# Experts in units of 512 gate or 512 up columns, own buffers for the last down weights, and a scatter in fp32r

## The chip, the cores and the metric

The kernel runs on one core of one Trainium2 chip, in one launch. The metric is the device time of that launch in microseconds. Engines: TensorE (PE, its weight loads PEld), VectorE (DVE), ScalarE (ACT), GpSimd (POOL) and SyncE (SP), which issues nearly all DMAs. A name with q (SPq) is the sequencer of an engine.

## The reference

Two transformer blocks on 256 tokens of 1,024 features, in fp32. The first block has two layers: attention and a dense SwiGLU of 3,584 columns, then attention and a mixture of eight SwiGLU experts. The second block adds a context stream, a SwiGLU of 2,816 columns for both streams (ff0c, ff0x), a long convolution, a differential attention, and a last SwiGLU (ff1). What matters here is the mixture:

```python
def moe_swiglu(h, router, wg, wu, wd):
    logits = (h @ router).astype(jnp.float32)
    top_vals, top_idx = lax.top_k(logits, TOP_K)          # 2 of 8
    gates = jax.nn.softmax(top_vals, axis=-1)
    gate_e = jnp.sum(jax.nn.one_hot(top_idx, N_EXPERTS, dtype=jnp.float32) * gates[..., None], axis=-2)
    out = jnp.zeros_like(h)
    for e in range(N_EXPERTS):
        out = out + gate_e[..., e:e + 1] * swiglu(h, wg[e], wu[e], wd[e])   # (silu(h @ wg) * (h @ wu)) @ wd
    return out
```

## The kernel before

**Products.** Weights come as fp32 and are multiplied as fp32r in three products: high x high, high x low, low x high. So each weight tile is split on the chip: ScalarE copies it to fp32r (the high part), VectorE subtracts that from the original (the low part).

**A block of a SwiGLU.** `feed` (on TensorE, ScalarE and VectorE, each with its own version) runs over blocks of 256 hidden columns (FB); an expert has NB1 = 14 of them, ff0c, ff0x and ff1 have NB2 = 11. The A tile of a block holds 256 gate and 256 up columns next to each other, 2 MB; it lands in `ringA` (two buffers) in two halves h of four row groups, each half as one DMA of gate and one of up with rows of 1 KB. The split halves lie in `As`, which has one buffer for each half. The B tile holds 256 rows of the down weights, 1 MB, lands in `ringB` (two buffers) and is split into `Bs` (one buffer).

**Order on TensorE.** In body n: `gu` of half 0 (12 matmuls of 512 columns), `turn` (two transposes of the hidden block n-1), `gu` of half 1 (12), `down` of block n-1 (12, added up in PSUM banks 4 to 7). For the experts there is one token tile (T = 1) of up to 128 gathered tokens; elsewhere there are two (T = 2), with twice as many matmuls for the same weights.

**Order on ScalarE in body n.** `hidden` (high part of the transposed block n-1), A half 0 of tile n+1 (L1497, waits A_lo_free, which TensorE raises after half 0), silu of block n (L1535), A half 1 of tile n+1 (waits tile_done), and B(n) into `Bs` (L1545, waits down_done of block n-1).

**Order on VectorE in body n.** `hidden` (low part, L2092, raises hdT_ready), A half 0 (L2077, raises A_split), silu times up (L2108), A half 1, B(n) (L2114, raises B_low), and then what `after(n)` adds: in bodies 2 and 3 the addition of the previous expert's rows to x (L2150), in body 3 the one-hot columns (`one_hot`, L2130 to L2137), in body 12 the gathered tokens (`dispatch`).

**Order on SyncE.** `load_experts` (L569 to L607) issues A(2i), B(2i-1), A(2i+1), B(2i) in a loop. A(n) waits for A_split of tile n-2, half by half; B(n) waits for B_low of block n-2. After the last expert `load_ffn` issues the loads of ff0c.

**Experts.** One expert follows the other without a break. For each, `gather` picks its tokens with one-hot matmuls. After its last down, `keep_y` (ScalarE, L1574, in body 1 of the next expert) copies the result out of PSUM and frees the banks (acc_free). `scatter` (TensorE, L884, after bodies 2 and 3 of the next expert) multiplies it in fp32 with `selgT`: the one-hot matrix that carries the gates, transposed by TensorE at block 12 (L897) and copied by ScalarE in body 13 (L1585).

**The end of a stage.** Where `drains` holds (dense, last expert, ff0x, ff1), the last block's `turn` and `down` stand alone behind body nb-1, with four idle products (L690) between them. Its Bs copy waits until the down before it is done. A second path for more than 128 tokens per expert (`all_tokens`) is in the program and is not taken with these inputs: the trace shows the gather of the first one.

## Time and profile before

| What | us |
|---|---|
| Median of 3 runs | 2700.34 |
| The runs | 2695.68, 3695.21, 2700.34 |
| The profiled execution | 2695.8 |
| Its span, first to last instruction | 2694.0 |
| TensorE busy in the span | 2573.2 (96%) |
| VectorE busy | 1820.4 (68%) |
| ScalarE busy | 1456.5 (54%) |

The span holds 34,481 instructions and the mean granted clock of TensorE is 0.975 of full speed. The mixture of experts runs from about 605 to 1643 us. The DMAs move 631.66 MB, of which the experts' weights are the greater part: 224 loads of gate and 224 of up with 512 KB each, 112 of down with 1 MB.

How to read it: a busy share is an average over stages with different limits. In a row of the timeline the first number is the start, the second the duration (of a group of like instructions, if xN is more than 1), and the brackets tell how long the engine was idle before it and what ended that. Matmuls overlap in the records, so the pace is read from start to start.

### The profile page before, as it was taken

The page shows a single profiled execution, that of the slowest core. Times are in us where ns is not written, and L with a number is a line of the kernel's source. Part 1 is how long each engine was busy: PE and PEld are TensorE (multiplying, and loading weights), DVE is VectorE, ACT ScalarE, POOL GpSimd, SP SyncE. Part 2 cuts the span into 40 slices and gives each one's busy share as a digit, 9 for nine tenths or more (in the row PEclk, how much of TensorE's full clock was granted, in tenths as well). Part 3 has the DMA queues.
Part 4 walks back from the last instruction along what each step waited for, and adds up shares of the span by engine and source line. Part 5 has one row for each costly group of instructions (what it writes and reads, how often), then busy time and mean ns, then how long its engine had stood idle before and what let it go on. Part 6 is the DMA issues. An engine that isn't in the chain of part 4 may idle for free.

```text
span 2694.0 us, 34481 instructions
## 1 busy us (share of the span) xinstructions
PE 2573.2 (96%) x11981; PEld 2031.8 (75%) x11981; DVE 1820.4 (68%) x1810; ACT 1456.5 (54%) x1677; POOL 52.2 (2%) x40
## 2 busy tenths in 40 slices
PE   7899999878999999999999998999999999998998
PEld 6678887656878787878888886888884687776786
DVE  6454446548888988888888885545444475776544
ACT  4544434535677777777777675445333243466443
POOL 0000000015000000000000000000000000000000
PEclk9999999879999999999999999999999999998999
DMA  6865542659999999999999996555543344435551
GB/s 217 290 219 187 187 156 87 241 179 308 367 336 353 348 351 349 352 349 351 349 346 355 339 343 203 181 185 184 183 156 108 102 142 127 130 107 179 184 186 60
DMA packets 446014, 631.66 MB, mean 234 GB/s; under 512 B 17672, under 2 KB 345896, under 8 KB 445736
## 3 DMA queue, kind: packets, MB, share of 16 engines
q1 hardware_dynamic: 445064, 627.36, 69.5%
q0 software_dynamic: 864, 3.15, 0.3%
q8 instruction: 55, 0.90, 0.1%
q14 instruction: 31, 0.25, 0.0%
HBM read 629.40 MB, written 1.05 MB: 234 GB/s over the span
## 4 chain that ended last, share of the span: by engine, by line
PE 87%; DVE 6%; ACT 4%; issue 2%; DMA 1%; SPq 0%; DVEq 0%; ACTq 0%
PE ps L806 39%; PE ps L834 20%; PE ps L1188 6%; PE ps L740 5%; PE ps L1215 2%; PE ps L1120 2%; PE ps L819 2%; PE ps L930 1%; PE ps L871 1%; DVE As L2077 1%; PE ps L1179 1%; DVE ringL L2047 1%; PE ps L884 1%; ACT Bs L1545 1%; ACT As L1497 1%
## 5 line engine op out<-in xcount | busy, mean ns | idle before, releaser
L2077 DVE TENSOR_TENSOR As<-ringA,As 128x2048 fp32r<-128x2048 f32 x318 | 735.2, 2312 | 212.4 <-ACT As L1497 203.5
L806 PE MATMUL ps<-As,xgs 128*128 128x512 f32 x2688 | 666.1, 397 | 6.7 <-DVE As L2077 4.1
L1497 ACT ACTIVATE As<-ringA 128x2048 fp32r<-128x2048 f32 x318 | 608.0, 1912 | 22.7 <-DMA ringA<-in_dense_w_up 9.9
L834 PE MATMUL ps<-Bs,hds 128*128 128x512 f32 x2472 | 590.0, 391 | 12.3 <-DVE hds L2092 12.3
L806 PEld LDWEIGHTS ps<-As,xgs 128*128 128x128 f32 x2688 | 494.7, 188 | 117.5 <-issue 14.3
L834 PEld LDWEIGHTS ps<-Bs,hds 128*128 128x128 f32 x2472 | 464.1, 188 | 116.5 <-issue 9.2
L2114 DVE TENSOR_TENSOR Bs<-ringB,Bs 128x2048 fp32r<-128x2048 f32 x159 | 368.8, 2320 | 157.4 <-ACT Bs L1545 156.8
L1545 ACT ACTIVATE Bs<-ringB 128x2048 fp32r<-128x2048 f32 x159 | 304.9, 1918 | 215.6 <-PE ps L834 215.4
L806 PE MATMUL ps<-As,xs 128*128 128x512 f32 x1632 | 392.3, 397 | 10.8 <-DVE xs L2015 6.8
L806 PEld LDWEIGHTS ps<-As,xs 128*128 128x128 f32 x1632 | 306.3, 190 | 78.3 <-issue 7.6
L1518 ACT ACTIVATE hds<-ps 128x256 fp32r<-128x256 f32 x206 | 73.9, 383 | 317.5 <-PE ps L819 282.8
L1535 ACT ACTIVATE sg<-ps 128x256 f32<-128x256 f32 x206 | 79.1, 384 | 192.9 <-PE ps L806 168.7
L2092 DVE TENSOR_TENSOR hds<-ps,hds 128x256 fp32r<-128x256 f32 x206 | 82.2, 418 | 90.1 <-ACT hds L1518 89.5
L2047 DVE TENSOR_TENSOR ringL<-ringA,ringH 128x2048 fp32r<-128x2048 f32 x42 | 96.1, 2290 | 57.3 <-ACT ringH L1477 57.1
L740 PE MATMUL ps<-As,xs 128*128 128x512 f32 (+1 forms) x384 | 118.7, 393 | 9.4 <-DVE ringL L2047 5.6
L2108 DVE TENSOR_TENSOR hh<-sg,ps 128x256 f32<-128x256 f32 x206 | 85.3, 415 | 55.8 <-ACT sg L1535 55.7
L1477 ACT ACTIVATE ringH<-ringA 128x2048 fp32r<-128x2048 f32 x42 | 80.2, 1911 | 79.2 <-PE ps L1188 57.7
L806 PE MATMUL ps<-As,hcTR 128*128 128x512 f32 x352 | 111.6, 398 | 0.0
L740 PEld LDWEIGHTS ps<-As,xs 128*128 128x128 f32 x384 | 73.8, 198 | 25.1 <-DVE ringL L2047 6.0
L1188 PE MATMUL ps<-ringL,hcTR 128*128 128x512 f32 x224 | 87.6, 391 | 0.0
L740 PE MATMUL ps<-ringL,xs 128*128 128x512 f32 (+1 forms) x224 | 87.2, 389 | 0.0
L1188 PE MATMUL ps<-ringH,hcTR 128*128 128x512 f32 x208 | 83.3, 401 | 0.8 <-DVE ringL L2047 0.8
(349 smaller groups left out, 2632.4 us busy)
## 6 DMA issues: line engine op xcount, KB each, us to landing
ringA<-in_moe_w_gate SPq DMA_DIRECT2D x224, 512.0 KB, 4.5
ringA<-in_moe_w_up SPq DMA_DIRECT2D x224, 512.0 KB, 5.6
ringB<-in_moe_w_down SPq DMA_DIRECT2D x112, 1024.0 KB, 6.2
ringA<-in_w_ff_in SPq DMA_DIRECT2D x132, 512.0 KB, 4.7
ringA<-in_w_in SPq DMA_DIRECT2D x56, 1024.0 KB, 5.3
ringA<-in_w_ada SPq DMA_DIRECT2D x36, 1024.0 KB, 6.2
ringB<-in_w_ff_out SPq DMA_DIRECT2D x33, 1024.0 KB, 5.0
ringA<-in_dense_w_gate SPq DMA_DIRECT2D x28, 512.0 KB, 3.6
```

Of the source, the lines that this page charges most:

```text
L740: m = mm(ps[:, 4 + 2 * (n % 2) + tt, 0:cols], xs[:, l, k, tt * P:(tt + 1) * P], w, start=k == 0 and m_ == 0, stop=k == KC - 1 and m_ == 2)
L806: m = mm(ps[:, bank, :], lhs(l, tt, k), As[:, h, r, k % 4, :], start=k == 0 and n == 0, stop=k == KC - 1 and n == 2)
L834: m = mm(ps[:, 4 + 2 * tt + half, :], hds[:, buf, l, q, :], Bs[:, q, r, half * 512:(half + 1) * 512], start=first and q == 0 and n == 0, s ...
L1188: m = mm(dst, lhs[l][:, k, tt * P:(tt + 1) * P], w[q], start=k == 0 and m_ == 0, stop=k == KC - 1 and m_ == 2)
L1477: A(high(p["name"], n, h)[:, :, 0:cols], ringA[:, a0 % 2, 4 * h:4 * h + 4, 0:cols], ACT.Copy).then_inc(A_high, 1)
L1497: A(As[:, h, 0, :, :], ringA[:, (p["a"] + u) % 2, 4 * h:4 * h + 4, :], ACT.Copy).then_inc(A_high, 1)
L1545: A(Bs[:, :, 0, :], ringB[:, b0 % 2, :, :], ACT.Copy).then_inc(B_high, 1)
L2047: V.tensor_tensor(ringL[:, a0 % 2, 4 * h:4 * h + 4, 0:cols], ringA[:, a0 % 2, 4 * h:4 * h + 4, 0:cols], f32(high(p["name"], n, h)[:, :, 0: ...
L2077: V.tensor_tensor(As[:, h, 1, :, :], ringA[:, (p["a"] + u) % 2, 4 * h:4 * h + 4, :], f32(As[:, h, 0, :, :]), ALU.subtract).then_inc(A_spli ...
L2092: V.tensor_tensor(flat(hds[:, buf, 1, :, :]), ps[:, 2 + tt, 0:FB], f32(flat(hds[:, buf, 0, :, :])), ALU.subtract).then_inc(hdT_ready, 2 // T)
L2108: V.tensor_tensor(hh[:, buf, :], sg[:, buf, :], ps[:, buf, FB:BW], ALU.mult).then_inc(h_ready, 2 // T)
L2114: V.tensor_tensor(Bs[:, :, 1, :], ringB[:, (p["b"] + u) % 2, :, :], f32(Bs[:, :, 0, :]), ALU.subtract).then_inc(B_low, 1)
```

## The change

1. Experts only: `load_experts` loads 512 gate columns as one tile (u = 0) and 512 up columns as the next (u = 1), each half with one DMA and rows of 2 KB. TensorE runs a new body: half 0, transposes of part u of the pair before, half 1, down of part u of the pair before. Silu and the product with up run once per pair over 512 columns. The down weights of block 2i+u are split in the body of unit 2i+1+u and used one unit later than before.
2. Where a stage drains, the last down weights are split into a place of their own (`down_home`): the high part into hTR or xs, the low part in place of the load in `ringB` (which ringH overlays). The idle products between are gone, and the downs of the block before are spread around the last transposes. For the experts' last pair this is done for its first part. The first B load of ff0c then waits until that part is done.
3. `selT` is now a matrix of 0 and 1 (VectorE compares the transposed selg with 0), the gate of each row is a sum in `small` (VectorE, `gate_sums`), `keep_y` scales by it and rounds to fp32r, `y_low` (VectorE) makes the rest and frees the banks, and `scatter` runs two fp32r matmuls for each half in place of one in fp32. `keep_y` moved from body 1 to body 2.

The path for more tokens (all_tokens) is changed in the same way. The core of the diff:

```diff
+        def down_home(p, b):
+
+            return by_rows(xs[:, 0, :, :] if p["name"] == "ff0x" else hTR[:, :, :]), by_rows(ringH[:, b % 2, :, :])
...
-        ye = ar(1024, D)
+        ye = arenaR[:, 1024:1024 + D], hTR[:, 0:4, :].rearrange("p k n -> p (k n)")
...
-        selgT = ar(2560, TILES, P)
+        selT = arenaR[:, 2560:2560 + TILES * P].rearrange("p (t s) -> p t s", t=TILES)
...
-                    n, a0 = i * 2 + u, p["a"] + u
-                    g, up = wg(e), wu(e)
+                    a0 = p["a"] + u
                     for h in range(2):
                         if isinstance(e, int) and isinstance(i, int) and i == 0:
                             half_free(a0, h)
                         else:
                             sp.wait_ge(A_split, e * (2 * nb) + i * 4 + (2 * (p["q"] + u) - 3 + h))
                         sl = slice(4 * h, 4 * h + 4)
-                        sp.dma_start(ringA[:, a0 % 2, sl, 0:FB], w2d(g)[:, sl, bass.ds(n * FB, FB)]).then_inc(A_full[a0 % 2][h], 16)
-                        sp.dma_start(ringA[:, a0 % 2, sl, FB:BW], w2d(up)[:, sl, bass.ds(n * FB, FB)]).then_inc(A_full[a0 % 2][h], 16)
+                        sp.dma_start(ringA[:, a0 % 2, sl, :], w2d((wg, wu)[u](e))[:, sl, bass.ds(i * BW, BW)]).then_inc(A_full[a0 % 2][h], 16)
...
-            load_ffn(ph["ff0c"], *g0)
+            load_ffn(ph["ff0c"], *g0, ring=(down_done, ph["ff0c"]["s"] - 2))
...
-                    if not lead:
+                    if last and drains:
+                        down(*prev, tts=(0,))
+                        turn(i, u)
+                        down(*prev, tts=(1,))
+                        down(i, u, weights=down_home(p, p["b"] + u))
+                    elif not lead:
                         down(*prev)
                     if after and isinstance(i, int):
                         after(2 * i + u)
-                    if last and drains:
-                        turn(i, u)
-                        idle_products(4)
-                        down(i, u)
...
-                    pe.wait_ge(selgT_ready, e + 1)
...
-                    last = mm(ps[:, 6 + half, :], selgT[:, tt, :], ye[:, half * 512:(half + 1) * 512], start=True, stop=True)
+                    for q in range(2):
+                        last = mm(ps[:, 6 + half, :], selT[:, tt, :], ye[q][:, half * 512:(half + 1) * 512], start=q == 0, stop=q == 1)
...
+                def body(i, u, last):
+                    lead = first and isinstance(i, int) and i == 0
+                    gate_or_up(e, i, u, 0, 1, lambda l, tt, k: xgs[:, l, k, :], 2 * e + 1, xg_split)
+                    if not lead:
+                        turn_part(e, i - 1, u, 1)
+                    gate_or_up(e, i, u, 1, 1, lambda l, tt, k: xgs[:, l, k, :], 2 * e + 1, xg_split)
+                    if last and final:
+                        down_part(e, i - 1, u, 1, qs=(0,))
+                        turn_part(e, i, 0, 1)
+                        pe.wait_ge(selgT_ready, e + 1)
+                        turn_part(e, i, 1, 1, 3, False)
+                        down_part(e, i - 1, u, 1, qs=(1,))
+                        down_part(e, i, 0, 1, down_home(moe, moe["b"]))
+                        down_part(e, i, 1, 1)
+                    elif not lead:
+                        down_part(e, i - 1, u, 1)
+                    if isinstance(i, int):
+                        after(2 * i + u)
+                blocks(pe, NB1, body, 2)
...
-                A(ye[:, :], ps[:, 4:6, :].rearrange("p a b -> p (a b)"), ACT.Copy).then_inc(acc_free, 1)
+                act.wait_ge(selgT_ready, e + 1)
+                A(ye[0], ps[:, 4:6, :].rearrange("p a b -> p (a b)"), ACT.Copy, scale=small[:, 354:355]).then_inc(y_high, 1)
...
+                def body(i, u, last):
+                    if isinstance(i, int):
+                        before(2 * i + u)
+                    lead = first and isinstance(i, int) and i == 0
+                    nxt = (i + 1, 0) if u else (i, 1)
+                    if not lead:
+                        part_high(e, i - 1, u, 1)
+                    unit_high(e, *nxt, 0)
+                    if last and not final:
+                        rows_part(e + 1, 0)
+                    if u == 0:
+                        gate_silu(e, i, 1)
+                    unit_high(e, *nxt, 1)
+                    if last and not final:
+                        rows_part(e + 1, 1)
+                    if last and final:
+                        down_high(e, i, 0, down_home(ph["moe"], ph["moe"]["b"])[0], 0)
+                        part_high(e, i, 0, 1)
+                        part_high(e, i, 1, 1, 3)
+                        down_high(e, i, 1, None, 2)
+                    elif u:
+                        down_high(e, i, 0)
+                    elif not lead:
+                        down_high(e, i - 1, 1)
+                blocks(act, NB1, body, 2)
...
+                def body(i, u, last):
+                    lead = first and isinstance(i, int) and i == 0
+                    nxt = (i + 1, 0) if u else (i, 1)
+                    if isinstance(i, int) and i == 1 and u == 0 and not first:
+                        y_low(e - 1)
+                    if last:
+                        gate_sums(e)
+                    if not lead:
+                        part_low(e, i - 1, u, 1)
+                    unit_low(e, *nxt, 0)
+                    if last and not final:
+                        rows_part(e + 1, 0)
+                    if u:
+                        gate_times_up(e, i, 1)
+                    unit_low(e, *nxt, 1)
+                    if last and not final:
+                        rows_part(e + 1, 1)
+                    if last and final:
+                        down_low(e, i, 0, down_home(ph["moe"], ph["moe"]["b"]))
+                        part_low(e, i, 0, 1)
+                        part_low(e, i, 1, 1, 3)
+                        down_low(e, i, 1)
+                    elif u:
+                        down_low(e, i, 0)
+                    elif not lead:
+                        down_low(e, i - 1, 1)
+                    if isinstance(i, int):
+                        after(2 * i + u)
+                blocks(dve, NB1, body, 2)
...
+            def gate_sums(e):
+
+                dve.wait_ge(selg_tp, e + 1)
+                V.tensor_reduce(small[:, 354:355], ps[:, 3, 0:TILES * P], X, ALU.add)
+                V.tensor_scalar(selT[:, :, :].rearrange("p a b -> p (a b)"), ps[:, 3, 0:TILES * P], 0.0, None, ALU.is_gt).then_inc(selgT_ready, 1)
+
+            def y_low(e):
+
+                dve.wait_ge(y_high, e + 1)
+                V.scalar_tensor_tensor(ye[1], ps[:, 4:6, :].rearrange("p a b -> p (a b)"), small[:, 354:355], f32(ye[0]), ALU.mult, ALU.subtract).then_inc(acc_free, 1)
```

## Rows read from the trace of the kernel before

**Rows 1.** Windows view, one expert: us, busy of each engine, TensorE clock, DMA share, GB/s.
```profile
859.80:986.00 126.20, 125.95 (x577) 102.21 (x576) 111.66 (x85) 90.57 (x75) 0.00 (x0) 1.00 1.02 350
```

**Rows 2.** Timeline of one block: start, us, engine, line, operation, count, idle before.
```profile
918.10 2.88 PE L806 MATMUL ps<-As,xgs 128*128 128x512 f32 x12
...
921.58 1.92 ACT L1497 ACTIVATE As<-ringA 128x2048 fp32r<-128x2048 f32 x1
...
923.52 2.29 DVE L2077 TENSOR_TENSOR As<-ringA,As 128x2048 fp32r<-128x2048 f32 x1 [0.65 <-ACT As L1497]
...
923.81 2.88 PE L834 MATMUL ps<-Bs,hds 128*128 128x512 f32 x12
...
926.05 0.37 SPq L582 DMA_DIRECT2D ringA<-in_moe_w_gate  x1
...
926.53 2.88 PE L806 MATMUL ps<-As,xgs 128*128 128x512 f32 x12
926.88 1.92 ACT L1545 ACTIVATE Bs<-ringB 128x2048 fp32r<-128x2048 f32 x1 [0.63 <-PE ps L834]
...
928.84 2.29 DVE L2114 TENSOR_TENSOR Bs<-ringB,Bs 128x2048 fp32r<-128x2048 f32 x1 [0.26 <-ACT Bs L1545]
...
931.38 0.37 SPq L590 DMA_DIRECT2D ringB<-in_moe_w_down  x1
```

**Rows 3.** Windows view: two microseconds of 1 KB rows, then two of 4 KB rows.
```profile
919.50:921.50 2.00, 2.00 (x11) 1.63 (x10) 1.56 (x2) 0.93 (x2) 0.00 (x0) 1.00 1.08 381
925.00:927.00 2.00, 2.00 (x11) 1.65 (x10) 1.87 (x3) 1.37 (x2) 0.00 (x0) 1.00 1.02 404
```

**Rows 4.** Timeline, end of the mixture stage: a B load, then A halves landing.
```profile
1611.85 0.38 SPq L590 DMA_DIRECT2D ringB<-in_moe_w_down  x1
...
1619.76 1.92 ACT L1497 ACTIVATE As<-ringA 128x2048 fp32r<-128x2048 f32 x1 [0.17 <-DMA ringA<-in_w_ff_in]
...
1624.11 1.91 ACT L1497 ACTIVATE As<-ringA 128x2048 fp32r<-128x2048 f32 x1 [1.46 <-DMA ringA<-in_w_ff_in]
```

**Rows 5.** Tile view of in_moe_w_down: time from issue to landing.
```profile
DMA to landing us min/median/max: 4.8/6.2/9.7
```

**Rows 6.** Timeline, units after the scatters of one expert.
```profile
1024.66 3.31 PE L806 MATMUL ps<-As,xgs 128*128 128x512 f32 x12
...
1034.83 3.31 PE L806 MATMUL ps<-As,xgs 128*128 128x512 f32 x12
...
1037.93 1.21 DVE L2150 TENSOR_TENSOR x<-x,ps 128x1024 f32<-128x1024 f32 x1
...
1040.79 0.41 DVE L2092 TENSOR_TENSOR hds<-ps,hds 128x256 fp32r<-128x256 f32 x1
...
1041.38 3.01 PE L834 MATMUL ps<-Bs,hds 128*128 128x512 f32 x12 [0.25 <-DVE hds L2092]
```

**Rows 7.** Chain of waits, end of dense and end of ff1: start, us, what.
```profile
400.65 5.47 PE ps L834 x24
...
408.68 1.28 ACT L1610
...
414.21 1.13 DVE x L2387
...
2670.76 5.47 PE ps L834 x24
...
2676.32 1.92 ACT Bs L1545
...
2680.94 3.07 PE ps L834 x12
...
2685.71 1.29 DVE xn L2735
```

**Rows 8.** Timeline, last block of the mixture stage.
```profile
1617.98 2.29 DVE L2114 TENSOR_TENSOR Bs<-ringB,Bs 128x2048 fp32r<-128x2048 f32 x1 [0.18 <-ACT Bs L1545]
...
1630.93 3.00 PE L834 MATMUL ps<-Bs,hds 128*128 128x512 f32 x12 [2.67 <-DVE hds L2092]
```

More of the change, by code:

```diff
@@ L381, in build @@
         ada("adar", 2, 16)
[L382 removed]
+        ffn("moe", NB1, NE, loads=1)
         ffn("ff0c", NB2)
@@ new lines, in turn_part @@
+            def turn_part(e, i, u, T, bank=2, follows=True):
+                for tt in range(T):
+                    pe.wait_ge(h_ready, ffn_count(moe, T, e, i, 1, tt))
+                    v = ffn_count(moe, T, e, i, u, tt, 1)
+                    if follows and started(v):
+                        pe.wait_ge(hdT_ready, v)
+                    for q in range(2):
+                        src = hh[:, u, q * P:(q + 1) * P] if T == 1 else hhW[:, tt, u * FB + q * P:u * FB + (q + 1) * P]
+                        m = tr(ps[:, bank if T == 1 else tt, q * P:(q + 1) * P], src, ident)
+                    m.then_inc(tp_done, 2 // T)
@@ new lines, in down_part @@
+            def down_part(e, i, u, T, weights=None, qs=range(2)):
+                first = isinstance(i, int) and i == 0 and u == 0
+                for tt in range(T):
+                    if first and tt == 0:
+                        pe.wait_ge(acc_free, e + moe["f"])
+                    pe.wait_ge(hdT_ready, ffn_count(moe, T, e, i, u, tt))
+                    if tt == 0:
+                        pe.wait_ge(B_low, e * NB1 + i * 2 + (moe["b"] + u + 1))
+                    for q in qs:
+                        for n, (l, r) in enumerate(((0, 0), (0, 1), (1, 0))):
+                            for half in range(2):
+                                m = mm(ps[:, 4 + 2 * tt + half, :], hds[:, u if T == 1 else tt, l, q, :], (Bs[:, q, r, :] if weights is None else weights[r][:, q, :])[:, half * 512:(half + 1) * 512],
+                                       start=first and q == 0 and n == 0, stop=q == 1 and n == 2, skip_group_check=True)
+                    if 1 in qs:
+                        m.then_inc(down_done, 2 // T)
@@ L862, in gather, with all_tokens @@
+            def all_tokens(e):
+                def body(i, u, last):
+                    for h in range(2):
+                        gate_or_up(e, i, u, h, 2, split_stream, 1, xr_split)
+                    if u:
+                        for part in range(2):
+                            turn_part(e, i, part, 2)
+                            down_part(e, i, part, 2)
+                blocks(pe, NB1, body)
             def gather(e):
@@ L1529, in body @@
                         split_rows(0)
+                    b0 = p["b"] + u
+                    if last and drains:
+                        act.wait_ge(B_full[b0 % 2], e * (8 * nb) + i * 16 + 16 * (b0 // 2 + 1))
+                        A(down_home(p, b0)[0], ringB[:, b0 % 2, :, :], ACT.Copy).then_inc(B_high, 1)
                     for tt in range(T):
@@ L1539, in body @@
                         split_rows(1)
-                    b0 = p["b"] + u
+                    if last and drains:
+                        hidden(i, u)
+                        return
                     act.wait_ge(B_full[b0 % 2], e * (8 * nb) + i * 16 + 16 * (b0 // 2 + 1))
@@ L1545, in body @@
                     A(Bs[:, :, 0, :], ringB[:, b0 % 2, :, :], ACT.Copy).then_inc(B_high, 1)
-                    if last and drains:
-                        hidden(i, u)
                 blocks(act, nb, body, head)
@@ new lines, in part_high @@
+            def part_high(e, i, u, T, bank=2):
+                p = ph["moe"]
+                for tt in range(T):
+                    act.wait_ge(tp_done, ffn_count(p, T, e, i, u, tt))
+                    v = ffn_count(p, T, e, i, u, tt, 3 - T)
+                    if started(v):
+                        act.wait_ge(down_done, v)
+                    A(hds[:, u if T == 1 else tt, 0, :, :].rearrange("p a b -> p (a b)"), ps[:, bank if T == 1 else tt, 0:FB], ACT.Copy).then_inc(hd_high, 2 // T)
@@ L2101, in body @@
                         split_rows(0)
+                    if last and drains:
+                        dve.wait_ge(B_high, e * nb + i * 2 + (p["b"] + u + 1))
+                        hi, lo = down_home(p, p["b"] + u)
+                        V.tensor_tensor(lo, ringB[:, (p["b"] + u) % 2, :, :], f32(hi), ALU.subtract).then_inc(B_low, 1)
                     for tt in range(T):
@@ L2440, in all_tokens, with body @@
                 def all_tokens(e):
-                    feed(p, 2, e, True)
+                    def body(i, u, last):
+                        nxt = (i + 1, 0) if u else (i, 1)
+                        if u:
+                            gate_times_up(e, i, 2)
+                        for h in range(2):
+                            unit_low(e, *nxt, h)
+                        if u == 0:
+                            down_low(e, i, 0)
+                        else:
+                            part_low(e, i, 0, 2)
+                            down_low(e, i, 1)
+                            part_low(e, i, 1, 2)
+                    blocks(dve, NB1, body)
+                    dve.wait_ge(down_done, e * (2 * NB1) + (p["s"] + 2 * NB1))
                     dve.wait_ge(acc_free, e + 1)
```

132 lines of the change are left out of this document (110 added, 22 removed).

## The prediction

> **What bounds the kernel now.** I read the windows view first, one window per expert. An expert of the middle of the mixture stage takes 126.2 us; TensorE is busy for 125.95 of them at full clock, VectorE for 111.66, and the DMA engines move 350 GB/s at a share of 1.02 [rows 1]. So TensorE sets this stage, eight experts long, and two others are close behind it. Which cover hides them, the timeline of one block tells [rows 2]. Count from the start of a block of 256 gate and 256 up columns (918.10). TensorE does 24 matmuls of gate and up, two transposes, 12 matmuls of down, and starts the next block at 926.53: 8.43 us a block. ScalarE splits the first half of the next tile from 921.58 (3.48 after the start), VectorE from 923.52 to 925.81, 0.7 us before the next block. VectorE's low part of the down weights runs at 928.84 to 931.13. SyncE reuses each buffer at once: the load of A's first half goes out at 926.05, that of B at 931.38. The rest of this text is about those slacks of half a microsecond.
>
> **The inner loop: nothing to gain on TensorE.** A unit is now 512 gate columns or 512 up columns, and two units make a pair. A pair has 48 matmuls of gate and up and 24 of down, as two blocks had; by [rows 2] it takes 2 x 8.43 us again. One silu and one product of 512 columns replace two of 256 each: some 0.2 us less per pair on ScalarE and on VectorE, both of which have idle time (126.2 - 111.66 = 14.5 us for VectorE in an expert [rows 1]). I cost it at nothing.
>
> **The loads: 1 KB rows become 2 KB rows, and SyncE's order turns against them.** The loads of A are half as many and longer; a stretch of 1 KB rows moves 381 GB/s, one of 4 KB rows 404 [rows 3]. The bytes stay. But the down matmuls of a unit now come one unit later: down_low for B(n) ran in VectorE's body n and now runs in body n+1. SyncE's program keeps its order: A(n+3) stands behind the load of B(n+1), which waits for that down_low. Before, the two A halves went out in the middle of the body (926.05 and 2.7 us later), ahead of B at 931.38. Now all three leave together, at 13.28 us from the start of unit n (931.38 - 918.10), with B first. Queued behind the waiting B are exactly A(n+3)'s two halves, and ScalarE waits for those. ScalarE wants A's first half in unit n+2, at 16.86 + 3.48 = 20.34, and VectorE's result then has about 0.45 us to spare: 2.29 us of work that begins 1.94 us after ScalarE's, with two handovers, against 8.43: of the 0.7 us that it ended early about 0.25 go into handovers. The budget from B's issue to A's landing is 20.34 + 0.45 - 13.28 = 7.5 us.
> What will it take? The trace has one such bunch, at the end of the stage: B goes at 1611.85, the first A half directly behind it, and ScalarE, which waited for it, starts at 1619.76, 7.9 us later; the second half follows at 1624.11 [rows 4]. That half was of 1 KB rows; at the rate of long rows 1.05 MB takes 2.60 us in place of 2.75, so 7.75. This is 0.25 to 0.3 over the budget, in a circle of two units (the bunch waits for TensorE's unit n, and TensorE's unit n+3 for the bunch; the down in between ties it to n+1), so 0.14 us a unit. Seven experts of 14 units give 98 x 0.14 = 14 us. Bounds: the quickest 1 MB load of B landed in 4.8 us [rows 5]; with 2.6 for the half behind it 7.4, so 0. The median is 6.2: 8.8 us, 1.3 over, 0.65 a unit, 64 us. I take 14, since the row of 1619.76 is the only one of this very order.
> The Trainium skill's page DMA: Bandwidth & Descriptors (Anatomy of one DMA) fits a transfer as 2.0 us plus its bytes at 436 GB/s. By that an estimate for both is 6.8 us, and the term would be 0; the bunch in [rows 4] took 7.9, so the trace is slower than the page here.
>
> **The scatter.** Each expert ends with two scatters of two fp32 matmuls. A block that follows one starts 10.17 us after the one before (1034.83 - 1024.66), so a scatter costs 10.17 - 8.43 = 1.74 us. Now it is four fp32r matmuls of 512 columns at 2.73/12 = 0.23 us: 0.92. That saves 0.82 twice per expert. VectorE pays for it. Added are y_low, a 128x1024 operation from PSUM like the 1.29 us of L2735 [rows 7], in unit 2 before part_low, and gate_sums (two passes over 256 columns, like the 0.41 of hds each [rows 6]) in unit 13. Removed is one ScalarE copy.
> Unit 2: B's low part starts 2.31 after the unit's start (928.84 - 926.53) and lasts 2.2 net of the overlap with the next row; y_low ends at 5.8, part_low at 6.2, TensorE sees it at 6.4. The down is due at 5.71 (923.81 - 918.10 [rows 2]): 0.67 us of wait. ScalarE's copy y_high (1.0 us, half of the 1.92 of the copy of 2048 columns at 926.88, behind its B copy that ends at 2.3) is hidden.
> Unit 4: before, the addition to x started 3.10 into the unit (1037.93), one-hot columns followed, and hds came at 1040.79; the down began at 1041.38 with 0.25 us of wait [rows 6]. The shorter scatter gives less time ahead of it: B's low part starts at 2.31 - 0.92 = 1.39, the addition at 3.6, hds at 3.6 + 2.86 = 6.46, ready at 7.05, due 5.71: 1.34 us. Scatter and waits cost 1.84 + 0.67 + 1.34 + 0.2 (gate_sums) = 4.05, before 3.48 + 0.25 = 3.73. Seven experts: +2 us. Bounds: no wait felt, 7 x -1.9 = -13; the same chain against a unit with A late, +6.
>
> **The ends of stages.** Dense, ff0x and ff1 end with a free-standing block: ScalarE's Bs copy waits for the last down (2676.32), VectorE follows, TensorE fills with idle products and starts the last down at 2680.94 [rows 7]. With an own buffer both parts are made earlier, under 11 us of gate and up. From 2670.76: down of one token tile 2.73, transposes 0.44, the other 2.73, so 2676.66: 4.3 us earlier in ff1 and in ff0x, which has the same chain. In dense another chain ends later: the next weights are split by ScalarE and VectorE before x is updated at 414.21. From 400.65 + 5.9 = 406.55 (the buffer of the second tile is free) 0.4 + 1.28 + 1.92 + 2.29 with handovers is 412.5, so 1.7 (0.4 for a part of 256 columns, 1.28 the table load at 408.68). Sum -10.3; bound -12.9, if dense gets all.
>
> **The end of the mixture stage** is where two edits meet. The last B load waited for down_low of block 11, done 1611.82. That now comes a unit later, at 1617.98 + 2.29 = 1620.27 [rows 8], less 2.73 because TensorE has done one down less by then: 1617.5. Behind it stand ff0c's first A loads, and ScalarE splits those before it touches down_home. With the bunch of [rows 4], the halves land 7.9 and 12.3 later, at 1625.7 and 1630.1. Then ScalarE: split to 1632.0, home copy to 1633.9, two parts, B copy to 1636.6; VectorE behind it: 1634.3, 1636.6, 37.0, 37.4, 1639.7; TensorE: down (6,0) at 37.1, down (6,1) at 1639.9. Before, the last down began at 1630.93 [rows 8]: 9.0 us later. y_low (1.3) lies under the three idle products; the last two scatters give 1.6 back. Term +7.4. Bounds: if the loads are in time, the same chain from 1621.7 ends 2.2 earlier, so -3.8; +9.
> The first expert has its own losses on VectorE while GpSimd works; the same operations stay, I cost it at 0, within 4 either way.
>
> **Sum.** -10.3 + 7.4 + 2 + 14 = +13. The profiled execution took 2695.8 us (span 2694.0), so 2709; it lay 4.5 below the median of 2700.34.
>
> **Rivals.**
> 1. The loads are in time. The inner loop holds 8.43; ends, scatter and drain as above: 2695.8 - 10.3 + 7.4 + 2 = 2695. For it: 2 KB rows, 7.4 us from the quickest loads. 0.27. The fit of the Trainium skill's page DMA: Bandwidth & Descriptors (Anatomy of one DMA) would give this case.
> 2. As 1, and VectorE's new work is hidden and the last drain is not held by loads: 2695.8 - 10.3 - 3.8 - 13 = 2669. Against it: 0.25 us of wait stood in unit 4 already. 0.10.
> 3. The other side: the bunch takes the median landing. Place: SyncE, A behind B in each unit. Price 64 us in place of 14: 2759. It decides from a landing of 8.6 us on, where 98 x 0.55 = 54 us is 2%. 0.15.
> 4. The change doesn't do what it says (fewer load instructions, no idle products): next to nothing, 0.03.
> The forecast itself: 0.45, with 2690 to 2735.
>
> **Numbers.** Range 2670 to 2759, from rival 2 to rival 3, leaves out about 0.2. Two per cent, about what a measurement of this kernel can tell, is 54 us. Faster by more: 0.02, since no case reaches 2646. Slower by more: most of rival 3, 0.13. Within: 0.85.
>
> **What would show it.** In the timeline of the middle of an expert, SyncE's issues stand in a bunch, B first, 13.3 us after the unit start (right or wrong at once); ScalarE's A copies name a DMA as what they waited for; TensorE's L806-like halves wait for As. Unit starts 8.43 apart there: rival 1. PE's waits for hds stand in units 2 and 4, 0.7 and 1.3 us. The last block of ff1 has no idle products and ends 4.3 us earlier against its gate and up. After the last expert's matmuls, ScalarE waits for in_w_ff_in before it copies down weights. Wrong it would be if the silu, longer by some 0.2 us, pushes A's second half over its slack of about half a microsecond, or if 2 KB rows start flowing sooner after their issue than 1 KB rows do.

## The result, and the profile after

The changed kernel takes 2710.41 us (median of 6 runs, 2708.38 to 2713.71), the kernel before 2698.34 in the same series (median of 5: a sixth run, of 3695 us, was disturbed and is left out): a ratio of 1.0047, 95% interval 1.0032 to 1.0063. So the change makes the kernel slower, by about half a per cent. The forecast was 2709.0, slower too, and within 2% of the kernel before. The profiled execution has a span of 2708.8 us, before 2694.0; the 14.8 us between these two are what the rows can explain.

To see where they lie, I cut both spans at the same instructions of TensorE: the start of the first gather, the two transposes of selg at the end of each expert (L897 before, L973 after), and the first matmul of ff0c, of ff0x (the first that reads hTR, 0.5 us after its very first) and of the convolution. One down (12 matmuls, 2.73 us) has moved from ahead of the expert's mark to behind it; the table puts it back.

| Stretch, us | before | after | difference | forecast |
|---|---|---|---|---|
| up to the first gather | 605.2 | 604.1 | -1.0 | -1.7 |
| first expert | 128.1 | 128.7 | +0.5 | 0 |
| the seven others | 882.5 | 901.0 | +18.5 | +16 |
| last mark to ff0c's first matmul | 32.7 | 37.4 | +4.8 | +7.4 |
| ff0c | 184.8 | 184.3 | -0.5 | 0 |
| ff0x with its end | 430.3 | 427.3 | -3.0 | -4.3 |
| the rest with ff1's end | 430.4 | 425.9 | -4.5 | -4.3 |

The windows view, one expert, answers to [rows 1]. The columns are the same.

```profile
988.43:1117.12 128.69, 126.18 (x575) 101.71 (x574) 111.44 (x80) 90.44 (x67) 0.00 (x0) 1.00 0.94 341
```

TensorE does the same number of matmuls at full clock and now stands still for 2.5 us in each expert (128.69 - 126.18), before for 0.25; the DMA share fell from 1.02 to 0.94. The timeline of the middle of an expert shows what it stands still for; it answers to [rows 2].

```profile
1189.64 0.37 SPq L602 DMA_DIRECT2D ringB<-in_moe_w_down  x1
...
1190.74 1.00 SPq L595 DMA_DIRECT2D ringA<-in_moe_w_gate  x2
...
1198.29 0.37 SPq L602 DMA_DIRECT2D ringB<-in_moe_w_down  x1
1198.31 1.92 ACT L1673 ACTIVATE As<-ringA 128x2048 fp32r<-128x2048 f32 x1 [1.17 <-DMA ringA<-in_moe_w_gate]
...
1200.26 2.29 DVE L2254 TENSOR_TENSOR As<-ringA,As 128x2048 fp32r<-128x2048 f32 x1 [1.90 <-ACT As L1673]
...
1202.61 3.06 PE L892 MATMUL ps<-As,xgs 128*128 128x512 f32 x12 [0.53 <-DVE As L2254]
...
1207.79 0.37 SPq L602 DMA_DIRECT2D ringB<-in_moe_w_down  x1
...
1208.90 1.00 SPq L595 DMA_DIRECT2D ringA<-in_moe_w_gate  x2
...
1211.22 2.88 PE L892 MATMUL ps<-As,xgs 128*128 128x512 f32 x12
```

Read it from left to right in time. B goes out at 1189.64 and A's two halves stand right behind it: the bunch. ScalarE has been waiting for 1.17 us when the gate half is there at 1198.31, 8.67 us after B's issue. VectorE's low part follows, and TensorE's unit starts 0.53 us late at 1202.61. The next unit starts 8.61 us after that, with no wait. Not every unit is late: of 97 distances between unit starts in the seven experts, 23 are over 0.25 us longer than the same ones of e1 (the same kernel without the bunch, below), 29 more by 0.1 to 0.25, and units 3 to 6 of an expert lose 0.2 us at the most.

The waits view of ScalarE and then of TensorE, from 735 to 1600 us (time in total, times, the longest). Before, TensorE's view of this stretch had one line, 1.5 us for hds. TensorE's 6.3 us for As are about a third of what the bunch costs; the rest doesn't show as a named wait (see e1).

```profile
ACT As L1673 <- DMA ringA<-in_moe_w_gate: 40.0, 51, 1.9
...
ACT As L1673 <- DMA ringA<-in_moe_w_up: 13.0, 25, 1.4
```

```profile
PE ps L922 <- DVE hds L2315: 10.1, 13, 1.1
PE ps L892 <- DVE As L2254: 6.3, 13, 1.2
```

The page's DMA issues (number, KB each, median from issue to landing) fit: an A half now takes 8.3 or 9.0 us, B 5.0.

```profile
ringA<-in_moe_w_gate SPq DMA_DIRECT2D x112, 1024.0 KB, 8.3
ringA<-in_moe_w_up SPq DMA_DIRECT2D x112, 1024.0 KB, 9.0
ringB<-in_moe_w_down SPq DMA_DIRECT2D x112, 1024.0 KB, 5.0
```

Units 2 and 4 after an expert's end, from the timeline; they answer to [rows 6].

```profile
1151.86 1.28 DVE L2430 SCALAR_TENSOR_TENSOR hTR<-ps,small,arenaR 128x1024 fp32r<-128x1024 f32 x1
...
1153.06 0.41 DVE L2315 TENSOR_TENSOR hds<-ps,hds 128x256 fp32r<-128x256 f32 x1
...
1153.60 3.01 PE L922 MATMUL ps<-Bs,hds 128*128 128x512 f32 x12 [0.59 <-DVE hds L2315]
...
1173.09 0.42 DVE L2315 TENSOR_TENSOR hds<-ps,hds 128x256 fp32r<-128x256 f32 x1
...
1173.69 3.00 PE L922 MATMUL ps<-Bs,hds 128*128 128x512 f32 x12 [1.06 <-DVE hds L2315]
```

y_low stands ahead of hds in unit 2 and TensorE waits 0.59 us; in unit 4 it waits 1.06. The forecast said 0.67 and 1.34.

The end of the mixture stage, from the chain of waits; it answers to [rows 4, 8].

```profile
1636.52 6.95 DMA ringA<-in_w_ff_in
...
1643.49 1.92 ACT As L1673
...
1647.64 0.69 DVE hh L2327
...
1648.38 1.11 PE ps L907 x4
...
1652.41 1.91 ACT Bs L1703
...
1654.35 2.30 DVE Bs L2334
...
1656.79 3.00 PE ps L922 x12
```

ScalarE waits until 1643.49 for ff0c's first half, as foreseen. VectorE's product with up (hh) stands in its program behind the low part of that same half, so the last transposes wait too, for 9.85 us, until 1648.38. The last down begins at 1656.79.

The end of ff1, from the chain of waits; it answers to [rows 7].

```profile
2690.02 2.74 PE ps L847 x12
2692.76 0.44 PE ps L831 x4
2693.20 5.52 PE ps L847 x24
...
2698.74 1.12 ACT xn L2151 x2
```

From the last gate and up to the norm it is 8.72 us; before, 13.27 (2670.76 to 2684.03).

### The profile page after: what moved, and what is told of

It reads as the page before. It is cut to its first block, busy times and chain, and to the rows that moved or that the text cites. A ratio compares the mean times of both kernels' runs of the same rounds, so it can differ in the third digit from the quotient of the medians.

```text
span 2708.8 us, 33553 instructions
## 1 busy us (share of the span) xinstructions
PE 2564.5 (95%) x11949; PEld 2026.9 (75%) x11949; DVE 1817.4 (67%) x1778; ACT 1455.6 (54%) x1613; POOL 51.2 (2%) x40
## 4 chain that ended last, share of the span: by engine, by line
PE 69%; DVE 12%; DMA 7%; ACT 6%; issue 5%; SPq 1%; DVEq 0%; ACTq 0%
PE ps L818 19%; PE ps L892 9%; PE ps L847 9%; DMA ringA<-in_moe_w_gate 6%; PE ps L1283 6%; PE ps L752 5%; PE ps L922 5%; DVE As L2254 4%; ACT As L1673 3%; DVE Bs L2334 2%; PE ps L1310 2%; PE ps L1215 2%; PE ps L1025 1%; PE ps L947 1%; PE ps L831 1%
## 5 line engine op out<-in xcount | busy, mean ns | idle before, releaser
L818 PEld LDWEIGHTS ps<-As,xs 128*128 128x128 f32 x1632 | 306.5, 190 | 75.5 <-issue 5.5
L922 PE MATMUL ps<-Bs,hds 128*128 128x512 f32 x1332 | 323.6, 392 | 11.8 <-DVE hds L2315 10.9
L922 PEld LDWEIGHTS ps<-Bs,hds 128*128 128x128 f32 x1332 | 249.5, 188 | 69.8 <-issue 17.6
L2334 DVE TENSOR_TENSOR Bs<-ringB,Bs 128x2048 fp32r<-128x2048 f32 x111 | 253.8, 2287 | 10.5 <-ACT Bs L1703 9.5
L847 PE MATMUL ps<-Bs,hds 128*128 128x512 f32 x1056 | 247.8, 390 | 0.0
L1703 ACT ACTIVATE Bs<-ringB 128x2048 fp32r<-128x2048 f32 x111 | 212.5, 1914 | 39.6 <-PE ps L922 39.1
L847 PEld LDWEIGHTS ps<-Bs,hds 128*128 128x128 f32 x1056 | 198.1, 188 | 41.8
L2298 DVE TENSOR_TENSOR Bs<-ringB,Bs 128x2048 fp32r<-128x2048 f32 x44 | 100.9, 2293 | 119.7 <-ACT Bs L1646 119.7
L1646 ACT ACTIVATE Bs<-ringB 128x2048 fp32r<-128x2048 f32 x44 | 84.3, 1916 | 135.4 <-PE ps L847 135.4
L1634 ACT ACTIVATE sg<-ps 128x256 f32<-128x256 f32 x94 | 36.1, 384 | 126.6 <-PE ps L818 125.6
```

The costliest lines, as they stand in the source:

```text
L818: m = mm(ps[:, bank, :], lhs(l, tt, k), As[:, h, r, k % 4, :], start=k == 0 and n == 0, stop=k == KC - 1 and n == 2)
L847: m = mm(ps[:, 4 + 2 * tt + half, :], hds[:, buf, l, q, :], w[:, half * 512:(half + 1) * 512], start=first and q == 0 and n == 0, stop=q = ...
L922: m = mm(ps[:, 4 + 2 * tt + half, :], hds[:, u if T == 1 else tt, l, q, :], (Bs[:, q, r, :] if weights is None else weights[r][:, q, :])[: ...
L1703: A(Bs[:, :, 0, :] if dst is None else dst, ringB[:, b0 % 2, :, :], ACT.Copy).then_inc(B_high, 1)
L2298: V.tensor_tensor(Bs[:, :, 1, :], ringB[:, (p["b"] + u) % 2, :, :], f32(Bs[:, :, 0, :]), ALU.subtract).then_inc(B_low, 1)
L2334: V.tensor_tensor(lo, ringB[:, (p["b"] + u) % 2, :, :], f32(hi), ALU.subtract).then_inc(B_low, 1)
```

## The experiments

Each kernel's ratio is to the kernel before on the same chip (median 2697.4 us in the first series, 2697.3 in the second). The stretches below are those of the table above, read in the same way from each kernel's profiled execution. e1 to e4 ran on one chip, e5 to e7 on another, and the changed kernel in a series of its own. A difference between two kernels can therefore be taken from the medians or from their ratios to the kernel before, and where the two disagree both are given.

| Kernel | median us | first gather | first expert | seven experts | end of mixture | ff0x | rest |
|---|---|---|---|---|---|---|---|
| before | 2698.3 | 605.2 | 128.1 | 882.5 | 32.7 | 430.3 | 430.4 |
| after | 2710.4 | 604.1 | 128.7 | 901.0 | 37.4 | 427.3 | 425.9 |
| e1 | 2691.5 | 599.5 | 126.1 | 883.1 | 37.7 | 430.4 | 426.0 |
| e2 | 2681.4 | 599.6 | 126.6 | 883.1 | 29.7 | 427.3 | 425.9 |
| e3 | 2736.1 | 604.9 | 132.0 | 917.1 | 34.9 | 430.4 | 430.5 |
| e4 | 2724.4 | 600.0 | 129.9 | 913.9 | 39.6 | 427.5 | 426.0 |
| e5 | 2686.3 | 604.0 | 126.2 | 885.0 | 29.2 | 429.7 | 426.0 |
| e6 | 2694.3 | 605.0 | 126.3 | 883.1 | 29.7 | 434.2 | 430.5 |
| e7 | 2679.3 | 603.6 | 125.5 | 882.3 | 28.5 | 426.9 | 426.3 |

### e1: A ahead of B on SyncE

The changed kernel with one difference: A(n+3) is issued ahead of B(n+1), whose wait ends later.

```diff
-                    with sp.Fori(1, nb // 2) as i:
-                        A(e, i, 0)
...
+                    with sp.Fori(1, m - 1) as i:
+                        A(e, i, 1)
                         B(e, i - 1, 1)
-                        A(e, i, 1)
+                        A(e, i + 1, 0)
                         B(e, i, 0)
```

> The changed kernel with one edit in SyncE's program of the mixture stage: the load of A(n+3) is issued ahead of that of B(n+1), so that A no longer stands behind a wait for down_low. Theory (the bunch of loads is what slows the inner loop): ScalarE's splits of A in the experts wait for no DMA any more, unit starts are 8.43 us apart again, an expert takes 126.4 us from gather to gather in place of 128.9 (before: 126.14, less 1.6 for the scatters, plus some 2 of waits for hds in units 2 and 4), six of them give 15 us, the first and the last expert some 2 to 3 more: about 2692 us against 2710. The end of the stage keeps its loss, since ff0c's loads still stand behind the last B. Rival (VectorE's added work, y_low and gate_sums, is what costs, and the loads only look late): the experts stay at 128 us or more, 2705 to 2710.

Measured: 2691.46 us, ratio 0.998 (0.997 to 0.999). In SyncE's timeline A's halves no longer leave right behind B; they go when their own buffers come free.

```profile
1190.53 0.37 SPq L602 DMA_DIRECT2D ringB<-in_moe_w_down  x1
1193.85 3.32 SPq L595 DMA_DIRECT2D ringA<-in_moe_w_up  x2
```

ScalarE's waits view names no DMA from 735 to 1600 us, and an expert takes 126.28 us by the windows view:

```profile
849.08:975.36 126.28, 124.78 (x576) 102.06 (x575) 111.73 (x80) 89.91 (x67) 0.00 (x0) 1.00 0.96 349
```

This settles the cause of the loss: seven experts take 883.1 us in place of 901.0, the kernel 18.9 less (18.1 by the ratios). Nothing but the order of issues on SyncE is different. Of the 17.8 us, TensorE stood still for 9.0 (901.0 - 882.2 against 883.1 - 873.4 in the windows view of the seven experts); the other 8.8 lie in its busy time, with as many matmuls at the same granted clock of 1.00. Part of that shows in the records: the 12 matmuls of a first half that starts after a pause take 2.88 us up to the next group in the mean, in e1 a first half takes 2.74. ScalarE waited for second halves too (29 of its 76 waits ended 10 us or more after B's issue), but TensorE's pauses for As are all ahead of a first half. What is left above before in the seven experts is 0.7 us, the scatter with its waits.

### e2: A ahead of B at the end of the stage too

e1, with ff0c's first two A tiles issued ahead of the experts' last two B loads.

```diff
                     B(e, m - 2, 1)
                     if not last:
                         A(e + 1, 0, 0)
+                    elif tail:
+                        tail(0)
                     B(e, m - 1, 0)
...
                 run(NE - 1, NE - 2, True)
+                if tail:
+                    tail(1)
                 B(NE - 1, m - 1, 1)
...
-            load_experts(ph["moe"], one(t["moe_w_gate"]), one(t["moe_w_up"]), one(t["moe_w_down"]))
+            load_experts(ph["moe"], one(t["moe_w_gate"]), one(t["moe_w_up"]), one(t["moe_w_down"]), lambda k: load_ffn(ph["ff0c"], *g0, part=k))
```

> As the run with A first, and also at the end of the stage: ff0c's first two A tiles are issued ahead of the last two B loads of the last expert. Theory: ScalarE doesn't wait for in_w_ff_in in the last block, the last down starts some 9 to 10 us earlier, and part of that reaches the end of the launch: about 2683 us. Rival (the end is set by the row of ScalarE and VectorE work in the drain, not by the loads): no more than 2 us better than the run with A first.

Measured: 2681.41 us, ratio 0.9946 (0.9927 to 0.9965). By the timeline the transposes of the last pair wait 1.12 us for hh instead of 9.85. TensorE then waits 2.69 us for hds, which VectorE makes behind its low parts of ff0c's A tile and of the down weights:

```profile
1615.20 0.65 PE L927 MATMUL ps<-c,hh 128*128 128x128 f32 x4 [1.12 <-DVE hh L2347]
...
1619.94 1.22 PE L942 MATMUL ps<-hTR,hds 128*128 128x512 f32 x2 [2.69 <-DVE hds L2335]
...
1624.39 2.93 PE L942 MATMUL ps<-Bs,hds 128*128 128x512 f32 x12
```

The end of the mixture stage takes 29.7 us in place of 37.7: the 8.0 us were the wait for in_w_ff_in. The medians are 10.0 us apart, the ratios 9.2, the profiled executions 10.4; of the latter 8.0 lie here and 3.1 in ff0x, where both kernels have the same instructions (last section), the other stretches make -0.7. This kernel is faster than the changed one and than the one before, than the latter by 0.35 to 0.73%.

### e3: the bunch alone, in the kernel before

The kernel before, with B(n+2) ahead of A(n+3): its 1 KB rows and its blocks stay, only the order on SyncE turns.

```diff
                     with sp.Fori(1, nb // 2) as i:
-                        A(e, i, 0)
                         B(e, i - 1, 1)
-                        A(e, i, 1)
+                        A(e, i, 0)
                         B(e, i, 0)
+                        A(e, i, 1)
```

> The kernel before, with one edit in SyncE's program of the mixture stage: B(n+2) is issued ahead of A(n+3), so all three transfers of a unit leave in a bunch at the end of VectorE's body n, as in the changed kernel; blocks of 256 gate and 256 up columns, rows of 1 KB and the old scatter stay. Theory: the bunch alone costs. A bunch of 1 KB rows took 7.9 us to A's first half against a budget of 7.5, so 0.2 to 0.3 us a unit, 98 units: 20 to 30 us, 2719 to 2729, and ScalarE's splits name in_moe_w_gate or in_moe_w_up as what they waited for. Rival (the loss needs the late down or the new VectorE work): 2699, as before.

Measured: 2736.11 us, ratio 1.0148 (1.0123 to 1.0173): 39 us more, where at most 30 were expected. The sign and the place were right, by ScalarE's waits view from 735 to 1600 us, which named no DMA before:

```profile
ACT As L1497 <- DMA ringA<-in_moe_w_up: 91.2, 113, 2.8
```

The seven experts lose 34.6 us, 0.35 in each of 98 blocks. The expectation took the bunch of [rows 4] at 7.9 us. In the blocks in which ScalarE waited for a first half, it started 8.3 us after B's issue (median of 41, 880 to 1480 us). With 8.3 in place of 7.9 the expectation's own sum, half of what is over 7.5 us in each of 98 units, gives 39 us.

### e4: 1 KB rows in the changed kernel

The changed kernel, with each A half loaded by two DMAs of 256 columns.

```diff
-                        sp.dma_start(ringA[:, a0 % 2, sl, :], w2d((wg, wu)[u](e))[:, sl, bass.ds(i * BW, BW)]).then_inc(A_full[a0 % 2][h], 16)
+                        for c in range(2):
+                            sp.dma_start(ringA[:, a0 % 2, sl, c * FB:(c + 1) * FB], w2d((wg, wu)[u](e))[:, sl, bass.ds(i * BW + c * FB, FB)]).then_inc(A_full[a0 % 2][h], 16)
```

> The changed kernel with the A loads of the experts cut into rows of 1 KB again (two DMAs of 256 columns for each half, same tile in ringA, same order). Theory: shorter rows move 381 in place of 404 GB/s, so A's first half lands 0.15 us later in each bunch, 0.07 a unit, and the second half 0.3 later: 7 to 15 us slower than the changed kernel, 2717 to 2725. Rival (row length does not matter while the bunch is late for its latency): 2710.

Measured: 2724.42 us, ratio 1.0108 (1.0088 to 1.0128), 14.0 above the changed kernel by the medians, 16.5 by the ratios and 12.9 in the rows of the seven experts. ScalarE's waits view of the same stretch:

```profile
ACT As L1674 <- DMA ringA<-in_moe_w_gate: 52.5, 58, 1.6
ACT As L1674 <- DMA ringA<-in_moe_w_up: 41.8, 63, 2.0
```

94 us of waiting in place of 53. Where ScalarE waited for the first half, it started 8.3 us after B's issue, as in e3; in the changed kernel the median of 31 such cases is 7.9. So rows of 2 KB, with half as many DMAs, bring the half 0.4 us sooner, and the bunch costs 0.18 us a unit instead of 0.31 (31.4 - 0.7 = 30.7 us over 98 units).

The Trainium skill's page DMA: Bandwidth & Descriptors (Specifications) gives 512 bytes as the least transfer for line rate. Rows of 1 KB and of 2 KB are both above it, and 14.0 us still lay between them in this kernel, though this includes that e4 issues twice as many DMAs.

### e5: the old scatter

e2 with fp32 scatters of selgT and the copied result; no y_low, no gate_sums.

```diff
-                    for q in range(2):
-                        last = mm(ps[:, 6 + half, :], selT[:, tt, :], ye[q][:, half * 512:(half + 1) * 512], start=q == 0, stop=q == 1)
+                    last = mm(ps[:, 6 + half, :], selgT[:, tt, :], ye[:, half * 512:(half + 1) * 512], start=True, stop=True)
```

> e2_a_first_end with the old scatter: four fp32 matmuls per pair, gates in the selection matrix, no division of the gated results into a high and a low part. Theory (the shorter scatter is worth little, since the next unit waits for the one-hots that VectorE writes, hds wait 0.6 to 1.1 us twice an expert): the scatters get about 0.8 us longer twice an expert, the waits of the following units for the one-hots go away, and the expert stays at 126.3 to 126.8 us; with 1.6 us more at the end of the stage 2681 to 2688. Rival (the scatter is worth its whole length on the path): an expert of 127.9 us, 2681.4 + 8 x 1.64 = 2694 or more.

Measured: 2686.28 us, ratio 0.9956 (0.9941 to 0.9971). The waits of TensorE for hds from 735 to 1600 us, first in e2 and then in e5:

```profile
PE ps L942 <- DVE hds L2335: 8.3, 13, 1.1
```

```profile
PE ps L942 <- DVE hds L2337: 1.5, 6, 0.3
```

The scatters are longer and the long waits are gone; the windows view gives e5's expert 126.50 us, e2's 126.29. Seven experts: 885.0 against 883.1, 1.9 us, where the matmuls alone save 11.5. The rival (an expert of 127.9 us) falls. At the end of the stage, where the expectation had 1.6 us more, e5 took 0.5 less (29.2 against 29.7). The medians are 4.9 us apart, the ratios 2.7 with intervals that overlap. The profiled executions are 8.2 apart, but 4.4 of that lie ahead of the first gather and 2.3 in ff0x, where both kernels have the same instructions, and I don't count those for the scatter. By its own rows the new scatter is worth some 1 to 2 us; by the medians it could be up to 5, and the runs don't settle which.

### e6: the old ends of dense, ff0x and ff1

e2, with the last down weights in the buffer Bs again and idle products in the wait.

```diff
-                    if last and drains:
-                        down(*prev, tts=(0,))
-                        turn(i, u)
-                        down(*prev, tts=(1,))
-                        down(i, u, weights=down_home(p, p["b"] + u))
-                    elif not lead:
+                    if not lead:
                         down(*prev)
...
+                    if last and drains:
+                        turn(i, u)
+                        idle_products(4)
+                        down(i, u)
```

> e2_a_first_end with the old ends of the two dense feeds and the first feed-forward stage: the last down tile loads into a buffer that gate and up used, with idle products in the wait. Theory (a home of its own for the last down tile is worth what the predicted terms say, 4.3 + 4.3 + 1.7 us): 2681.4 + 10.3 = 2692 (2689 to 2695). Rival (those ends are hidden by what follows): 2680 to 2684.

Measured: 2694.28 us, ratio 0.9983 (0.9973 to 0.9992), 12.9 above e2 by the medians, 10.0 by the ratios. The chain of waits at ff1's end is that of [rows 7] again:

```profile
2670.57 5.47 PE ps L867 x24
...
2676.12 1.92 ACT Bs L1659
...
2678.06 2.29 DVE Bs L2306
...
2680.74 3.03 PE ps L867 x12
```

The last stretch takes 430.5 us in place of 425.9, 4.6 more; in dense it is 22.7 us from the last gate and up to the next stage's first matmul (400.50 to 423.22), in e2 21.2 (397.77 to 418.92). The seven experts take 883.1 in both. So the ends are worth what was said, and nothing hides them. ff0x's stretch is 6.9 us longer (434.2 against 427.3), more than the 4.5 of its end. That, like the 2.6 us of the medians beyond 10.3, is of the size by which stretches with equal instructions differ (last section).

### e7: the one-hot columns over two units

e2, with the one-hot columns of this expert in body 2 and those of the next in body 3.

```diff
-                    if n == 3:
+                    if n == 2:
...
-                        if not final:
-                            dve.wait_ge(gathered, 2 * e + 2)
-                            one_hot(e + 1, 2 * e + 3, False)
+                    if n == 3 and not final:
+                        dve.wait_ge(gathered, 2 * e + 2)
+                        one_hot(e + 1, 2 * e + 3, False)
```

> e2_a_first_end with VectorE's writing of the one-hot matrices spread over two units instead of one. Theory (what is left of the expert's loss is VectorE's bunch of work ahead of hds in units 2 and 4): the wait of unit 4 for hds falls from 1.06 us to 0.5 or less, an expert becomes 125.6 to 126.0 us, 2677 to 2680. Rival (the other work of VectorE in that unit, or the unit's own order, sets the wait): 2680 to 2683, with the wait as long in another unit.

Measured: 2679.27 us, ratio 0.9936 (0.992 to 0.9952); 2.1 below e2, with intervals that overlap, so not shown to be faster than e2. TensorE's waits view from 735 to 1600 us:

```profile
PE ps L942 <- DVE hds L2335: 5.6, 18, 0.4
```

The long waits are gone (longest 0.4 us in place of 1.1), but there are more of them, and an expert takes 126.15 us (mean of six, mark to mark) in place of 126.28: less than expected. Part of VectorE's work still stands ahead of hds, in another unit. It is the fastest kernel of the study by its median.

## Why the prediction was right, term by term

**The inner loop, 0.** Right. In e1, where no load is late, units without extra work start 8.43 us apart, and the seven experts differ from before by 0.7 us in all.

**The bunch, +14; measured 17.8 in the seven experts (901.0 - 883.1), and 2.6 more in the first.** The mechanism was right: the order on SyncE, ScalarE waiting for a half, TensorE's unit late. The sign that it named came too: B goes out at 1198.29, 13.33 us after the unit that starts at 1184.96 (13.3 in the prediction). The term was undersized: 0.18 us a unit in the mean and not 0.14, and the first expert was left out. The landing itself was well sized. ScalarE started 7.9 us after B's issue in the median of the units that waited, with 7.6 at the least and 8.67 in the case shown; by the landing times in the trace, all 93 bunches from 735 to 1600 us had the first half 7.50 to 10.06 us after B's issue, 7.78 in the median; I had 7.75. What was missing is the tail above the median (the mean is 7.98), and that TensorE's matmuls are slower after a pause (e1). The even loss in a circle of two units is only the rough picture: units 3 to 6 of an expert lose next to nothing, units 7 to 12 up to 1.4 us at a time. How much each of these made of the 0.04 us is not shown. The rates of [rows 3] gave 0.15 us for the longer rows, and e4 measured 0.4 (with twice as many DMAs): the rate of a busy stretch did not tell what a bunch gains from them. By the lower bound (4.8 + 2.6 = 7.4) the term would have been 0, by the median of [rows 5] 64. The only row of this very order was the right one to take.
The fit of the Trainium skill's page DMA: Bandwidth & Descriptors (Anatomy of one DMA) made this 6.8 us and the term 0; it is a fit of transfers that GpSimd issues, and SyncE issues these. None of the 93 bunches had less than 7.50, so here the measurement decides against it.

**Scatter and VectorE, +2; measured +0.7 (e1).** The waits were 0.59 and 1.06 us where I had 0.67 and 1.34, so the loss per expert is 0.1 us and not 0.3. That a scatter 0.82 us shorter is eaten by VectorE's work behind it was right, as e5 shows: the old one costs 1.9 us more in seven experts and not 11.5.

**The ends of stages, -10.3; measured -10.7 by their own rows.** ff1 4.55 (13.27 to 8.72), ff0x 4.5 (2015.53 to 2031.49 before, 2037.84 to 2049.29 after), dense 1.6 (400.65 to 423.38 before, 399.18 to 420.30 after). In dense another chain does end later, as the step said. e6 put the old ends back and lost 12.9 by the medians, 10.0 by the ratios.

**The end of the mixture stage, +7.4; measured +4.8.** The late load was sized well: B goes 4.53 us after the mark (the prediction's 1617.5 is 4.5 after the mark of before, 1615.76, less 2.73) and ScalarE has ff0c's first half 7.91 us later (7.9). The last down begins 25.74 us after the mark, before 15.17; less the 2.73 of the moved down that is 7.8 later, where I had 9.0. Two errors of the chain pull against each other here. It had the transposes done early, while in fact hh waits behind VectorE's low part of the same late half; that step was wrong. And it had the second half 12.3 us after B's issue, while ScalarE started on it after 10.93 (1646.51 - 1635.58).
From the start of the last down to ff0c's first matmul it is 14.42 us, before 17.48, so 3.1 saved instead of 1.6. The scatters give 1.5 of that, as priced. The rest lies behind the last addition to x, in a place that the prediction does not name. The timeline before and after:

```profile
1641.70 1.22 DVE L2150 TENSOR_TENSOR x<-x,ps 128x1024 f32<-128x1024 f32 x1 [2.15 <-PE ps L884]
...
1645.95 2.00 ACT L1507 ACTIVATE xs<-hcT 128x1024 fp32r<-128x1024 f32 x2 [10.96 <-DVEq L2453]
```

```profile
1666.18 1.22 DVE L2363 TENSOR_TENSOR x<-x,ps 128x1024 f32<-128x1024 f32 x1 [1.35 <-PE ps L960]
...
1668.12 2.00 ACT L1602 ACTIVATE xs<-hcT 128x1024 fp32r<-128x1024 f32 x2 [7.19 <-DVEq L2723]
```

ScalarE's copy for ff0c waits for a signal that VectorE's sequencer sends once it has left the If around the mixture stage: 4.25 us after the addition's start before, 1.94 after. From its branch instruction to the signal it is 2.9 us in the kernel before and in e3, 0.6 us in the changed kernel and in e1, e2 and e4 to e7. e5 has the old scatter, so these 2.3 us don't come from the scatter; why the branch takes less in the changed program is not shown. 0.6 us are lost again between that copy and ff0c's first matmul (3.1 us, before 2.5; e5 has 2.5 too).
e2 took the wait for in_w_ff_in away and -3.0 remains, near the bound of -3.8, but that is luck. The bound had the last down 2.2 us earlier than before; in e2 it starts 15.07 us after the mark (the moved down taken off), before 15.17, so 0.1 earlier. The other 2.9 lie behind it (14.62 us, before 17.48), and most of them are the branch. With the loads in time, the own place for the down weights gained 0.1 us at this end.

**The first expert, 0; measured +0.5.** Two things cancel: without the bunch (e1, e2, e5, e6) it is 1.5 to 2.1 us shorter than before. TensorE's waits for hds in it fell from 5.6 us to 1.8 (e2), those for As rose from 4.1 to 7.4; what makes up the rest is not shown.

**The rivals.** The loads in time (2695): e1 made that case true by itself and came to 2691.5. All hidden (2669): no; e5 and e7 show that VectorE's work stays on the path. The median landing (2759): no, but e3 shows how near it was, since the same order with 1 KB rows costs 39 us. The terms' errors (+3.8 in the experts, -1.3 in the scatter, -2.6 in the end, +0.5, -0.4 in the ends of stages) cancel, and what is left of the 1.7 us between 14.8 and 13.1 lies in stretches whose matmuls did not change. A forecast 1.4 us off the median is luck in its size; the direction, the place and the order of the terms were not.

## What to carry to other kernels

When a consumer moves one step later, look at the queue that issues the loads: the load that reuses its buffer now waits longer, and everything written behind it in that queue waits too. Here two such places cost 19 and 10 us by the medians, more than the change gained, and reordering the issues by the time at which their waits end gave both back. Price a shortened operation by what follows it: where the next unit waits for another engine, as in these experts, most of the saving becomes a wait (1.9 us left of 11.5).

## What the runs showed of the hardware

Stretches with the same instructions took 3 to 5 us more or less from one execution to the next, and TensorE's granted clock went with it. Up to the first gather, e1, e2 and e4 took 599.5, 599.6 and 600.0 us at a mean granted clock of 0.934, the changed kernel, e5 and e7 604.1, 604.0 and 603.6 at 0.924, 0.929 and 0.926. In the same way 50 us that begin 189 us after ff0x's first matmul, where its last downs end and the next steps begin; the windows view, first e1, then e2:

```profile
2020.00:2070.00 50.00, 45.84 (x131) 22.07 (x130) 18.80 (x36) 15.72 (x28) 0.00 (x0) 0.93 0.42 133
```

```profile
2012.80:2062.80 50.00, 45.84 (x138) 22.24 (x136) 18.79 (x36) 17.93 (x29) 0.00 (x0) 1.00 0.43 138
```

The granted clock (third column from the end) is 1.00 in e2, the level of 2.4 GHz throughout, and 0.93 in e1, so part of that stretch ran at 1.2 GHz; TensorE was busy for 45.84 us in both and for all of the 189 us before. ff0x's stretch took 430.4 and 427.3 us. An effect of 3 us in one profiled execution therefore needs its own rows, as the ends above have, and not a difference of spans.

SyncE does not issue a DMA directly behind another: in the bunches shown the issue of the first A half starts 0.65 to 1.11 us after the start of B's, which itself takes 0.37.
